# Cleared-tile matmuls on TensorE while a diffusion block's modulation weights are loaded

## The reference

```python
mod = jax.nn.silu(c) @ w_mod[l] + b_mod[l]
sh1, sc1, gt1, sh2, sc2, gt2 = jnp.split(mod[:, None, :], N_MOD, axis=-1)
mod_c = jax.nn.silu(c_ctx) @ w_mod[l] + b_mod[l]
h_lat = modulate(x, norm1_g[l], sh1, sc1)      # rmsnorm(x, g) * (1 + scale) + shift
h_ctx = modulate(ctx, norm1_g[l], csh1, csc1)
p_lat = h_lat @ w_in
p_ctx = h_ctx @ w_in
```

## Time and profile before

| | us |
|---|---|
| median of 3 runs | 2054.04 |
| lowest and highest of them | 2053.08 and 2056.02 |
| the profiled execution's own time | 2053.87 |
| its span, first to last instruction | 2052.6 |
| TensorE busy in it | 1973.3 (96%) |
| mean granted clock in it | 0.997 |

### The profile page before, as it was taken

How to read it: one execution, slowest core, us unless ns; L and a number is a source line. 1 busy time by engine, 2 the same in 40 slices (tenths; PEclk the granted TensorE clock), 3 DMA queues, 4 the chain that set the end, 5 groups by cost and what they waited for, 6 DMA issues and landing times.

```text
span 2052.6 us, 28312 instructions
## 1 busy us (share of the span) xinstructions
PE 1973.3 (96%) x11235; PEld 1606.9 (78%) x11235; DVE 1111.3 (54%) x1799; ACT 928.3 (45%) x1841; POOL 803.6 (39%) x448
## 2 busy tenths in 40 slices
PE   6989999989999999999999999999999999999998
PEld 5857787868777777878788888888677777788886
DVE  5578767775565657774544431346654565711114
ACT  3475757574455544223444433244534443522222
POOL 1212222213434315464344444443563551744442
PEclk9999999999999999999999999999999999999999
DMA  7245262623321216665332334345122323332332
GB/s 298 74 157 164 90 198 79 209 91 117 117 57 52 63 42 256 227 223 173 95 94 91 103 98 133 104 129 155 42 74 62 93 52 101 131 108 92 103 103 72
DMA packets 92323, 242.43 MB, mean 118 GB/s; under 512 B 28192, under 2 KB 31392, under 8 KB 90784
## 3 DMA queue, kind: packets, MB, share of 16 engines
q1 hardware_dynamic: 88784, 231.98, 35.7%
q10 hardware_dynamic: 3408, 8.65, 1.1%
HBM read 223.14 MB, written 14.29 MB: 116 GB/s over the span
## 4 chain that ended last, share of the span: by engine, by line
PE 61%; DVE 7%; ACT 2%; POOL 2%; issue 1%; DMA 1%; SPq 0%; DVEq 0%; ACTq 0%; POOLq 0%
PE ps L863 16%; PE ps L865 16%; PE ps L864 16%; PE ps L1232 2%; PE ps L1219 1%; PE ps L1207 1%; PE ps L1316 1%; PE ps L997 1%; PE ps L998 1%; PE ps L999 1%; PE ps L1275 1%; PE ps L1296 1%; DMA modr<-in_w_mod 1%; ACT whi L1362 1%; PE ps L921 1%
## 5 line engine op out<-in xcount | busy, mean ns | idle before, releaser
L2727 POOL TENSOR_TENSOR wlo<-raww,whi 128x1024 fp32r<-128x1024 f32 (+3 forms) x245 | 571.3, 2339 | 885.9 <-ACT whi L1362 874.5
L1362 ACT CAST whi<-raww 128x1024 fp32r<-128x1024 f32 (+2 forms) x279 | 279.1, 1006 | 173.2 <-PE ps L865 158.3
L863 PE MATMUL ps<-hT_h,whi 128*128 128x512 f32 (+1 forms) x688 | 257.5, 374 | 1.5 <-ACT rstd L1554 0.7
L864 PE MATMUL ps<-hT_l,whi 128*128 128x512 f32 (+1 forms) x688 | 250.6, 364 | 0.0
L865 PE MATMUL ps<-hT_h,wlo 128*128 128x512 f32 (+1 forms) x688 | 250.5, 364 | 0.0
L863 PE MATMUL ps<-H_h,whi 128*128 128x512 f32 x480 | 189.4, 395 | 2.4 <-ACT Pf L1397 2.4
L865 PE MATMUL ps<-H_h,wlo 128*128 128x512 f32 x480 | 187.0, 390 | 0.0
L864 PE MATMUL ps<-H_l,whi 128*128 128x512 f32 x480 | 187.0, 390 | 0.0
L863 PEld LDWEIGHTS ps<-hT_h,whi 128*128 128x128 f32 x688 | 129.9, 189 | 26.0 <-issue 4.0
L864 PEld LDWEIGHTS ps<-hT_l,whi 128*128 128x128 f32 x688 | 130.0, 189 | 21.1 <-issue 1.4
L865 PEld LDWEIGHTS ps<-hT_h,wlo 128*128 128x128 f32 x688 | 129.8, 189 | 21.2
(11 more groups left out here) (553 smaller groups left out, 4560.3 us busy)
## 6 DMA issues: line engine op xcount, KB each, us to landing
ec<-csd SPq DMA_DIRECT2D x32, 1024.0 KB, 7.9
raww<-in_w_up SPq DMA_DIRECT2D x44, 512.0 KB, 3.7
modr<-in_w_mod SPq DMA_DIRECT2D x32, 512.0 KB, 5.6
raww<-in_w_xbc SPq DMA_DIRECT2D x24, 512.0 KB, 3.6
raww<-in_w_gl SPq DMA_DIRECT2D x24, 512.0 KB, 3.6
raww<-in_w_z SPq DMA_DIRECT2D x16, 512.0 KB, 4.3
raww<-in_w_g SPq DMA_DIRECT2D x16, 512.0 KB, 3.6
raww<-in_w_os SPq DMA_DIRECT2D x16, 512.0 KB, 4.0
```

The source lines that it names most:

```text
L863: e.matmul(o, whi[:, i, c], hi(k)[:, t0:t1], start=(k == 0), stop=False)
L864: e.matmul(o, whi[:, i, c], lo(k)[:, t0:t1], start=False, stop=False)
L1362: e.copy(o, x.rearrange("p (k c) -> p k c", c=64) if p == plan.first["dt", 0] else x).then_inc(*w_high.mark(("high", p)))
L2727: e.tensor_tensor(o, x, h.bitcast(F32), ALU.subtract).then_inc(*p_wlow.mark(("split", p), ("raw free", p)))
```

## The change

A bf16 tile `blank`, 128 partitions by 512, is added at an address that nothing else uses at that time, and GpSimd clears it as its first step. TensorE's program gets 44 matmuls of this tile by itself (128 weight columns, 512 moving columns, PSUM bank 0, result read by nobody) as its very first work, and three more ahead of each of the four pieces of block 2, and two ahead of each of the other twelve pieces: 44 + 12 + 24 = 80 in all. The ones ahead of a piece stand before the wait for its landing.

```diff
+        blank = sbuf("blank", [P, 512], 204, BF16)
...
                 if k == "init":
+                    PE.wait_ge(at("blank"))
+                    for _ in range(44):
+                        e.matmul(ps[:, 0, :], blank[:, 0:128], blank[:, :], start=True, stop=True)
                     PE.wait_ge(at("constants"))
...
                     PE.wait_ge(at("silu c"))
                     w = mod_piece(j, n)[1]
+                    for _ in range({2: 3, 0: 2, 3: 2, 1: 2}[j]):
+                        e.matmul(ps[:, 0, :], blank[:, 0:128], blank[:, :], start=True, stop=True)
                     PE.wait_ge(at("modulation landed", j, n))
...
                 if k == "init":
+                    e.memset(blank[:, :], 0.0).then_inc(*p_made.mark(("blank",)))
                     e.memset(power[:, :], -0.5).then_inc(*p_step.mark())
```

## The result

| | before | the change |
|---|---|---|
| median, us | 2054.05 (10 runs) | 2059.36 (10 runs) |
| lowest and highest | 2053.08, 2056.02 | 2054.81, 2060.45 |
| the profiled execution's own time | 2053.87 | 2057.52 |
| its first product with w_in starts | 38.38 | 40.17 |

The ratio is 1.0022, 95% interval 1.0012 to 1.0032: the change is slower by about 0.2%, where no measurable difference was forecast and the range ended at 2057.0 us.

A forecast was written before the change was run, and what follows sets the result against it. The opening was taken as bound by DMA at its beginning and from about 32 us, with added matmuls hidden. From 2053.87 us, 0.4 us saved after piece 15 gave 2053.5, or 2053.6 us as median; range 2051.0 to 2057.0 us.

The forecast's parts named there:

- the price of a piece: Opening, TensorE at the high clock: a piece costs 0.50 us, two added matmuls ahead of it 0.44 us.
- the clock taken as high from piece 0 on: From 17.22 to 37.41 us TensorE was priced at the high clock, added matmuls at 0.22 us each.
- Pieces 5 to 8 at 0.94 us each: After the spread, from 26.0 us: four pieces with their added matmuls, done at 29.8 us.
- the spread: TensorE step after piece 4 and a turn: 1.42 us, ending at 26.0 us instead of 28.25.
- the spare 0.8 us: TensorE's spare time before piece 15 lands at 37.41 us: 0.8 us, up to 1.6 us without a piece's tail.
- The first rival: Clock falls between the 44 matmuls and piece 0: time from no loss to 2057 us; chance 0.25.
- the lead block: The 44 matmuls at the start take 11.3 to 13 us, done between 12.6 and 14.3 us, before piece 0.
- the likeliest case: Whole kernel: 2053.6 us, no measurable difference, the 44 matmuls covered by the 17.22 us wait for the first load; chance 0.59.
- the clearing of the tile: GpSimd's memset at the start: between 0.10 and 1.39 us, taken as 0.6 us, and free.
- tiles of zeros raising the clock: Rival at the 44 matmuls: clock stays low under zeros, 2073 us, 0.9% slower; chance 0.04.
- That gain of 0.4 us: After piece 15, at the high clock, the first product follows in 0.50 to 0.57 us, not 0.97; 0.45 us, taken as 0.4.
- The hv step: VectorE's hv starts some 2.2 us earlier than at 28.29 us, which buys nothing at the end.

## Why the prediction was wrong

**Two steps failed: the price of a piece, and the clock taken as high from piece 0 on.** The first makes the first product start 1.1 us later than forecast (39.0 us and not 37.9), the second 2.5 us later still (41.5 us in the mean of five traces). "Pieces 5 to 8 at 0.94 us each", made of 0.50 us for a piece and 0.44 us for two added matmuls, measured 1.11 us. Both prices were averages inside long rows of one kind; a piece alone, followed by something else, holds TensorE for 0.58 us (28.02 to 28.60 us), and two added matmuls followed by a piece for 0.53 us. With landings 1.28 us apart, 0.17 us more per step halves what TensorE gains on them. In the first trace with the gap filled the spread ends 0.46 us later than forecast (by 26.46 us and not 26.0), and the way from there to the first product takes 12.7 us, where the forecast's own prices without waits add up to 11.1 us. Together that is 2.0 us, more than the spare 0.8 us: with the clock high throughout, the first product is at 39.14, 38.94 and 38.92 us, 0.6 us later than the 38.4 us of before, and not 0.4 us earlier.

**The first rival came true each time.** It had a chance of 0.25. In all five traces of the change the clock fell near piece 0, after 2.81 to 3.95 us without work, in two of them only 0.9 and 1.6 us after piece 0 had begun, and stayed low for 3.4, 3.4, 6.8, 10.2 and 10.2 us. Filling the gap removed it in three traces of three, and in a fourth with fewer matmuls ahead of the pieces. The rival's formula took half of the low time after 19.6 us less 0.8 us of spare time. Against the 39.0 us with the clock high, the low time made the first product later by 1.2, 0.9, 2.6, 4.0 and 3.7 us. Half its length would be 1.7, 1.7, 3.4, 5.1 and 5.1 us; the part that is missing fell into idle time, such as the 0.5 us for which the filled kernels wait for `acc` ahead of the total. The five first products, at 40.17, 39.94, 41.64, 42.98 and 42.70 us, have a mean of 41.5 us: 3.1 us later than before. In time, filling the gap took away 5.0 of the 5.4 us that the change cost on the second chip. But the low clock costs this only where the added matmuls have used up the idle time: with the lead block alone 10.2 us of it cost nothing. The Trainium skill, "TensorE: Matmul & The Clock Gate", section "HAM oscillation", warns of waits between bursts that bring the half rate back; by that, the gap was the place to look at, and the traces agree. The 44 matmuls were done at 13.8 us as forecast (12.6 to 14.3), but in the likeliest case the gap behind them was taken as cover and not as a risk.

**What held.** The start at 1.31 us (1.3), the clearing of the tile at 0.53 us (0.6) and hidden, the lead block 12.53 us (11.3 to 13), and tiles of zeros raising the clock (nine of the 44 touch the window from 4 to 7 us, fifteen that from 10 to 13 us), and 0.58 us from the last piece to the first product at the high clock instead of 0.97. That gain of 0.4 us exists; the kernel with the lead block alone has it, at 37.88 us, but so has the one with nothing added before piece 15. The hv step came 0.6 us earlier and not 2.2, without effect.

**The range.** It was set from one trace and three runs that lay within 3 us. Later runs of the unchanged kernel went from 2052.0 to 2060.1 us. The price of a low stretch, 1.7 us, was known, but only the two of that one trace were counted.

**The sum, and what stays open.** In the traces the change's first product is 3.1 us later. Against that, in three of four traces of before the stretch that began near 34 us runs on beyond the first product: windows from 38.4 to 42.4 us have a clock of 1.00, 0.56, 0.79 and 0.72, 0.9 us lost on average, which the change doesn't lose. That leaves 2.2 us, and the mean spans of five and four traces, 2058.0 and 2055.7 us, differ by 2.3 us. That the two agree is partly luck: the traces come from several chips, and three of the four of before took longer than is usual, as said above.

The timed runs differ by more in the mean, 4.5 us on the first chip and 5.4 us on the second. Their granted clock is on record, and there the estimate (1 - clock) times the time is 10.8 us for the 25 runs of before on the second chip, 15.0 us for the change and 8.8 us for the kernel with the gap filled. From the traces the same estimate is 12.8, 13.7 and 6.8 us. So of the 5.4 us some 4.2 us are recorded low clock, where the traces show 0.9 us: those of before hold more of it than its timed runs do, and those of the change less. Where the timed runs of the change have the rest, in a longer opening or in more later stretches, stays open.

## What to carry to other kernels

A warm-up block should reach up to the first real work: with fillers between the pieces, twelve more matmuls took away 5.0 us of loss that 44 with a gap of 3 us had. Fillers ahead of waits must be priced as they stand, alternating with the real work, against the interval of the arrivals, because where they use up the idle time most of every later loss of clock goes to the end. Before that, look at what there is to gain: here it was 0.4 us, and no variant was measurably faster than the kernel before. A kernel whose runs differ by 3 us needs several traces before one of them is taken for the rule.

## What the runs showed of the hardware

- Idle times of TensorE ahead of piece 0 of 2.04 to 3.95 us, after a dense block of 44 to 50 matmuls, were followed by the low clock in all eight traces that had them; 0.30, 0.91, 1.18 and 1.31 us, after 59, were not.
- The low stretches that the granted clock shows up to 2000 us are 3.4, 6.8 or 10.2 us long. Where one may start, the same instructions after the same idle time (1.6 us) can go either way: near 231, 337 and 443 us two of the four traces of before kept the clock at all three places and two lost it at all three.
- The granted clock reads 1.00 up to its first recorded fall, also while matmuls take 421 ns as at the low level. For the opening the durations have to be read.
